# Gates in DRAM by groups of four keys instead of by halves of a tile

## The reference, cut to what matters

```
q = (tb @ wq).reshape(tokens, 8 heads, 2, 128)
s = einsum("thid,hikd->thik", q, keys)             # 128 keys on each of two sides
sv, si = top_k(s, 16)
comb = sv[:, :, 0, :, None] + sv[:, :, 1, None, :]   # 16 x 16 sums of a head
fv, fi = top_k(comb, 16); eidx = first * 128 + second
w = softmax(fv)
act = gelu(einsum("thkd,td->thk", u[eidx], tb))
out = einsum("thk,thkd->td", w * act, v[eidx])
```

## Time and profile before

| what | value |
|---|---|
| median of three runs | 5736.1 us |
| the profiled execution | 5734.65 us |
| its span | 5732.9 us |
| gate stage, first to last store's issue | 3380.40 to 3636.65 us |
| expert stage | about 3652 to 5660 us |
| TensorE busy over the span | 82% |
| VectorE busy over the span | 64% |
| TensorE, VectorE busy from 4160 to 4660 us | 484.90 and 481.79 us of 500 |
| DMA engines busy from 4160 to 4660 us | 98%, 363 GB/s |
| ten stores of the gates, 4096 KB each | 11.1 to 11.8 us from issue to landing |
| 32 loads of the gates, 1280 KB each | 11.0 to 15.9 us from issue to landing |

### The profile page before, as it was taken

How to read it: one execution, slowest core, us unless ns; L and a number is a source line. 1 busy time by engine, 2 the same in 40 slices (tenths; PEclk the granted TensorE clock), 3 DMA queues, 4 the chain that set the end, 5 groups by cost and what they waited for, 6 DMA issues and landing times. The chain is left out here.

```text
span 5732.9 us, 83257 instructions
## 1 busy us (share of the span) xinstructions
PE 4712.3 (82%) x28607; PEld 4320.5 (75%) x28607; DVE 3661.4 (64%) x6858; ACT 1812.0 (32%) x3649; POOL 1507.0 (26%) x1356
## 2 busy tenths in 40 slices
PE   5899999956665686988498746699999999999995
PEld 4899999944444444887387645688999998999994
DVE  2100035556666343223469977699999999999997
ACT  0111123323332233111144358533333333333332
POOL 0000000001111000000000000266777767777763
PEclk8999999978777566999799879899999999999998
DMA  2233222222211312334299713699999999999995
GB/s 97 99 115 114 96 82 92 101 78 98 89 72 73 59 25 61 126 121 157 94 374 339 264 63 143 249 357 346 352 372 366 357 363 360 354 364 371 356 356 209
DMA packets 342330, 1169.80 MB, mean 204 GB/s; under 512 B 40544, under 2 KB 85728, under 8 KB 337504
## 3 DMA queue, kind: packets, MB, share of 16 engines
q0 software_dynamic: 147456, 536.94, 25.3%
q1 hardware_dynamic: 156672, 483.22, 24.1%
q10 hardware_dynamic: 38112, 148.52, 6.8%
HBM read 971.35 MB, written 197.46 MB: 204 GB/s over the span
## 5 line engine op out<-in xcount | busy, mean ns | idle before, releaser
L1888 POOL DMA_INDIRECT ex_ur<-scr_u_rows,ex_at x512 | 614.4, 1200 | 320.5 <-DVE ex_ur L2065 146.4
L1890 POOL DMA_INDIRECT ex_vr<-in_expert_v,ex_at x512 | 614.2, 1200 | 265.7 <-issue 145.9
L2073 DVE SCALAR_TENSOR_TENSOR ex_acc_rows<-ex_vr,ex_wt,ex_acc_rows 128x1024 f32<-128x1024 f32 x512 | 649.6, 1279 | 38.7 <-ACT ex_wt L1993 37.3
L2065 DVE SCALAR_TENSOR_TENSOR ex_ur<-ex_ur,h_rows 128x1024 f32<-128x1024 f32 x512 | 619.1, 1218 | 2.9 <-DMA ex_ur<-scr_u_rows,ex_at 2.9
L1882 POOL COPY ex_at<-picked_at 128x4 uint32 x128 | 79.6, 622 | 1833.1 <-POOLq L117 1832.6
L803 POOL TENSOR_TENSOR sd_cts<-sd_cT,sd_ea 128x512 f32<-128x512 f32 x72 | 93.3, 1295 | 1726.0 <-ACT sd_ea L768 1726.0
L395 DVE TENSOR_TENSOR pr_w_lo<-pr_w,pr_w_hi 128x1024 fp32r<-128x1024 f32 x74 | 90.7, 1225 | 689.8 <-ACT pr_w_hi L391 689.8
L1900 PE MATMUL ex_ps<-hd_hi,ex_u_hi 128*128 128x320 f32 x2048 | 469.7, 311 | 28.4 <-DVE ex_u_lo L2039 25.8
L1900 PE MATMUL ex_ps<-hd_lo,ex_u_hi 128*128 128x320 f32 x2048 | 467.4, 309 | 0.0
L1900 PE MATMUL ex_ps<-hd_hi,ex_u_lo 128*128 128x320 f32 x2048 | 467.4, 309 | 0.0
L1991 ACT ACTIVATE ex_gel<-ex_dot 128x1 f32<-128x1 f32 x512 | 103.9, 203 | 983.4 <-DVE ex_ur L2065 983.4
(11 more groups left out here) (356 smaller groups left out, 11055.5 us busy)
## 6 DMA issues: line engine op xcount, KB each, us to landing
pk_raw_u<-in_expert_u SPq DMA_DIRECT2D x128, 512.0 KB, 6.4
scr_u_rows<-pk_rows_u ACTq DMA_DIRECT2D x128, 512.0 KB, 6.2
ex_u<-in_expert_u SPq DMA_DIRECT2D x128, 512.0 KB, 6.9
ex_v<-in_expert_v SPq DMA_DIRECT2D x128, 512.0 KB, 9.8
scr_gate<-gt_stage SPq DMA_DIRECT2D x10, 4096.0 KB, 11.2
ex_gate<-scr_gate SPq DMA_DIRECT2D x32, 1280.0 KB, 13.1
pr_w<-in_w_main SPq DMA_DIRECT2D x74, 512.0 KB, 4.7
scr_plain<-pr_out ACTq DMA_DIRECT2D x42, 576.0 KB, 3.1
```

The costliest lines, as they stand in the source:

```text
L1888: nc.gpsimd.indirect_dma_start(out=ur[:, s], out_offset=None, in_=scr["u_rows"], in_offset=by).then_inc(ur_in[s], 16)
L1890: nc.gpsimd.indirect_dma_start(out=vr[:, s], out_offset=None, in_=io["expert_v"].rearrange("j i d -> (j i) d"), in_offset=by).then_inc(vr_ ...
L2065: v.scalar_tensor_tensor(out=ur[:, s], in0=ur[:, s], scalar=1.0, in1=rows[:, s], op0=ALU.mult, op1=ALU.mult, accum_out=dot[:, m:m + 1]).th ...
L2073: v.scalar_tensor_tensor(out=acc_g[:, s], in0=vr[:, s], scalar=wt[:, m:m + 1], in1=acc_g[:, s], op0=ALU.mult, op1=ALU.add).then_inc(row_r[ ...
```

## The change

The DRAM tensor of the gates is laid out as `[p, group of 4 keys, half, key in the group, token]` instead of `[p, half, key, token]`. A load of four keys for all ten halves is then one run of 10 x 4 x 64 floats = 10 KB in each partition, where it was ten runs of 1 KB. A store of one half with its 128 keys is 32 runs of 1 KB in each partition, where it was one run of 32 KB. The bytes of each load and store, their number and the tiles in SBUF stay as they are. The constants `E`, `GB` and `GE` move to the top of the file with the same values.

```diff
+E, GB = 2, 2
+GE = GB * E
...
-                    sp.dma_start(scr["gate"][:, ds(t * 2 + h, 1)].rearrange("p h k t -> p (h k) t"), stage[:, h]).then_inc(stored[h], 16)
+                    sp.dma_start(scr["gate"][:, :, ds(t * 2 + h, 1)].rearrange("p g h e t -> p (g h) (e t)"),
+                                 stage[:, h].rearrange("p (g e) t -> p g (e t)", e=GE)).then_inc(stored[h], 16)
...
-    E = 2
     BATCHES = N_KEYS // E
...
-    GB = 2
-    GE = GB * E
...
-                    sp.dma_start(gate[:], scr["gate"][:, :, ds(g * GE, GE)]).then_inc(gate_in, 16)
+                    sp.dma_start(gate[:].rearrange("p h e t -> p (h e t)"), scr["gate"][:, ds(g, 1)].rearrange("p g h e t -> p (g h e t)")).then_inc(gate_in, 16)
...
-            ... "gate": dram("scr_gate", [P, TD // HALF, N_KEYS, HALF]), ...
+            ... "gate": dram("scr_gate", [P, N_KEYS // GE, TD // HALF, GE, HALF]), ...
```

More of the change, by code:

```diff
@@ L2220, in build @@
             "attn": dram("scr_attn", [ATTN // P, P, T]), "merged": dram("scr_merged", [KD, P, T]), "branch": dram("scr_branch", [KD, P, T]),
-            "x1": dram("scr_x1", [KD, P, T]), "gate": dram("scr_gate", [P, TD // HALF, N_KEYS, HALF]), "u_rows": dram("scr_u_rows", [N_KEYS * P, D]),
+            "x1": dram("scr_x1", [KD, P, T]), "gate": dram("scr_gate", [P, N_KEYS // GE, TD // HALF, GE, HALF]), "u_rows": dram("scr_u_rows", [N_KEYS * P, D]),
         }
```

## The result

The changed kernel takes 5699.32 us (median of eight, 5692.37 to 5705.36) against 5732.15 (median of eight, 5715.48 to 5761.89): a ratio of 0.994, 95% interval 0.9919 to 0.996. It is faster by about 0.6%. The profiled execution took 5694.76 us.

What follows compares the result with a forecast made beforehand. VectorE and TensorE were taken as nearly full in the expert stage, with VectorE losing 43.4 us to late gate loads. 5734.65 - 44.7 (expert stage) + 2.4 (last store) gave 5692 us; forecast's range 5680 to 5714, 8-in-10 range 5676 to 5726.

Steps and rivals of the forecast that it cites:

- Who waits, and the floor: Expert stage: VectorE waits 43.4 us for gates; 30 pairs at 60.23 us each leave at most 53.6 us to gain.
- the ruler: Expert stage: time between successive gate-load issues, one for each pair of batches; 60.23 us in a pair without gate wait.
- The sign that went with it: Expert stage after the change: nearly all pairs would take 60.2 to 60.5 us, with a few of 63.
- The load: Gate load in the expert stage: 10 KB packets, alternating one for one with q0's, land in 8.9 us; 11.74 are allowed.
- The tail: End of the gate load's landing: 1.2 us added to 3.4 us of work ahead and 4.3 us of packets.
- Rivals 1 and 2: Gate load: queues share by bytes, 5722 us, chance 14%; or run length does not matter, 5737 us, chance 7%.
- The store: End of the gate stage: 1 KB packets lengthen only the last, uncovered store, 2.4 us once, bounds 0 and 14.6.
- What follows a gate wait: Expert stage: 8.3 us beyond the gate waits follow them, TensorE being held after VectorE; they go with the waits.
- late gathers: Expert stage: gathered rows of `u` become late next, 10.7 us at worst, 2.9 already there; 7 us given back.
- one such wait in eight pairs without a gate wait: Expert stage: a 2.34 us wait for `ex_ur`, used to price late rows at 2.77 us, once in eight pairs.
- The forecast expert stage, -44.7: Expert stage: 51.7 us gained less 7 given back makes 44.7 us, bounds 35 and 54.6.
- rival 3: Expert stage: large gate packets starve the gathers, so VectorE waits for rows instead; slower, 5771 us, chance 5%.

Runs made afterwards that it cites:

- groups_5k: The change with its DRAM layout cut in two by half of a tile: loads of two 5 KB runs, stores of 1 KB runs; 5672.44 us, ratio 0.9907.
- change_again: The changed kernel as it is, measured again on the same chip as `groups_5k`; 5692.52 us, ratio 0.9943 to before.
- two_slots_groups: The change with groups of two keys in two slots, 640 KB loads issued a batch ahead, stores of 512 B runs; 5695.8 us, ratio 0.9953.
- mid_groups: `two_slots_groups` with the gate load moved between the two loads of `u`, mid-batch; 5682.48 us, ratio 0.9928.
- mid_halves: `mid_groups` with the DRAM layout of before: stores of 32 KB runs, loads of ten 512 B runs a partition; 5676.14 us, ratio 0.9908.
- load_5k: The change with stores of 32 KB runs and loads of two 5 KB runs a partition, gates of other tokens; 5677.3 us, ratio 0.9907.

## Why the prediction was right, step by step

- **Who waits, and the floor.** Right. VectorE's wait for gates was the term, and the ruler reads 60.22 us in the best pairs after against 60.23 before. The sign that went with it, 60.2 to 60.5 for nearly all pairs, did not come: three pairs did reach the floor and most lay at 60.4 to 61.4. With 5 KB runs it came.
- **The load.** Right in mechanism and size: 8.9 us forecast, 9.1 measured, with packets one for one in the microsecond shown. The tail was put at 1.2 us "as in the stores", which have 11.2 - 9.8 = 1.4; with that the sum is 9.1. Rivals 1 and 2 are excluded by the landing, by the 70% share, and by the landings at 5 and 2 KB.
- **The store.** 2.4 us forecast, once; SyncE's wait rose from 10.6 to 13.1 and the gap to the first load by 2.7. Nine of ten stores are covered: 256.25 and 256.29 us from the first issue to the last. The source was the row of gates almost alone, 336 packets in a microsecond. The estimate made from the Trainium skill, "DMA: Bandwidth & Descriptors", section on why small descriptors are slow (about 3 cycles of overhead for a packet), was 0.9 us; the landing rose from 11.2 to 13.8, and these 2.6 us disagree with it.
- **What follows a gate wait.** 8.3 us beside the waits. With the change this can't be told apart: few pairs are at the floor. In `groups_5k` neither a gate wait nor a late row is left in 27 pairs, and they are within 0.15 us of it; so it does go when both kinds of wait are gone.
- **The term that was mis-sized: late gathers.** I gave back 7 us, from one such wait in eight pairs without a gate wait, and took it as a matter of chance. The 30 pairs lie 1830.25 - 1806.9 = 23.4 us above the floor, where the forecast left 53.6 - 43.7 = 9.9. That is 13.5 us too little. The forecast expert stage, -44.7, came out at -32.8, below its own bound of 35. Two things were wrong. The price came from a row that says nothing of it: the 2.34 us of batch 34 recur without any gate load, so neither a chance of one in eight nor 2.77 us a case could be read from them. And the cost that did come is rival 3's mechanism at a small size. I gave it 5% as an alternative, when it was a term of the sum: the faster gates make the fourth row of `u` late. Without gate loads 16.1 us vanish, and with 5 KB runs 16.8 (`groups_5k` against `change_again`) at the same bytes. The listed waits for rows, 15.7 us, are two thirds of the 23.4; the rest is spread in pairs over the floor by less than 1 us and isn't traced further.
- **The total.** 5692 forecast, 5699.32 measured, inside the range. Faster by under 1% was the likeliest case and came. The profiled execution, 5694.76, looks closer than the forecast was: 9.8 us of its gain lie ahead of the first store and are luck. From there on 42.3 us were forecast and 30.1 came; the medians differ by 32.8.

## What to carry to other kernels

A transfer has a deadline in the timeline, here 11.74 us after its issue; it is enough to meet it. In this kernel speed beyond that was taken from the gathers that share the engines, so the largest packet was not the best: pick the one that just meets the deadline (5 KB here), or make the deadline loose with a second slot in the same space and place the load where no other transfer is tight. When a change gives one queue more turns, look up which transfer of the other queue has least slack, and put its wait into the sum. Before a single late transfer is used as a price, see whether it is late for the reason that is priced: one at the same place in every version is not.

## What the runs showed of the hardware

- A contiguous run of 10 KB in a partition is one DMA packet: in the microsecond shown 28 packets carried 0.29 MB. So is one of 32 KB: 128 packets carried 4.19 MB.
- A store of 4 MB in 32 KB packets lands in 11.2 us, in 1 KB packets in 13.8, and in 512 B packets (`two_slots_groups`, `mid_groups`) in 16.1. `two_slots_groups` was expected to be 5 to 10 us over the 1 KB runs.
- A two-slot load with 512 B packets, twice the count of before's, slowed nothing that could be measured (`mid_halves` against `mid_groups`). The engines' busy share is no sign of trouble: it was 0.98 before and 0.97 with the change.
- The issue of a store with 4096 rows holds SyncE for 0.54 to 0.69 us, against 0.33 to 0.37 for 128 rows. It isn't in proportion to the rows: the gate load takes 0.56 us with 1280 rows (before) and with 256 (`load_5k`).
